# Cross attention's keys and queries as 512-wide paired products, their halves added by VectorE

## The reference, cut to what matters

```python
def cross_attention(h, mem_n, wq, wk, wv, wo):
    b, s, _ = h.shape          # 1, 256, 1024
    m = mem_n.shape[1]         # 256
    q = (h @ wq).reshape(b, s, XATTN_HEADS, XATTN_DIM)      # 4 heads of 256
    k = (mem_n @ wk).reshape(b, m, XATTN_HEADS, XATTN_DIM)
    v = (mem_n @ wv).reshape(b, m, XATTN_HEADS, XATTN_DIM)
    sc = jnp.einsum('bshd,bmhd->bhsm', q, k).astype(jnp.float32) * (XATTN_DIM ** -0.5)
    p = jax.nn.softmax(sc, axis=-1).astype(v.dtype)
    o = jnp.einsum('bhsm,bmhd->bshd', p, v).reshape(b, s, XATTN_HEADS * XATTN_DIM)
    return o @ wo
```

## Time and profile before

| what | value |
|---|---|
| time, median of 3 runs (lowest, highest) | 2178.57 us (2178.45, 2178.62) |
| the profiled execution's own time | 2178.50 us |
| its span in the trace | 2176.6 us |
| TensorE busy | 2161.1 us, 99% of the span |
| VectorE, ScalarE busy | 1475.3 us (68%), 1116.0 us (51%) |
| keys to values, layer by layer | 1339.5 to 1421 us, and 1883.2 to 1965 us |

### The profile page before, as it was taken

The page is one execution under the profiler, slowest core; times in us unless marked ns, Lnnn a source line. Parts: engine busy times, 40 slices in busy tenths (PEclk is TensorE's granted clock), DMA queues, the critical chain, the costliest instruction groups (busy, mean ns, idle before and its releaser), DMA issues.

```text
span 2176.6 us, 31492 instructions
## 1 busy us (share of the span) xinstructions
PE 2161.1 (99%) x13360; PEld 1869.0 (86%) x13360; DVE 1475.3 (68%) x1624; ACT 1116.0 (51%) x1395; POOL 44.7 (2%) x46
## 2 busy tenths in 40 slices
PE   8999999999999999999999999999999999999998
PEld 7998888888999888888898888988889888898887
DVE  6778677655777868666678777456657877745654
ACT  5555565454564565545466535444446653544442
POOL 0000000000000000000000100000000010000000
PEclk9999999999999999999999999999999999999999
DMA  8555564655664456556564445456556444445652
GB/s 277 169 166 169 173 232 155 212 193 172 199 181 158 156 205 211 174 190 207 164 205 128 146 150 161 154 165 195 193 167 208 130 144 152 160 153 167 193 192 77
DMA packets 248754, 380.80 MB, mean 175 GB/s; under 512 B 22495, under 2 KB 158693, under 8 KB 248614
## 3 DMA queue, kind: packets, MB, share of 16 engines
q1 hardware_dynamic: 248614, 378.78, 54.0%
HBM read 372.26 MB, written 1.05 MB: 172 GB/s over the span
## 4 chain that ended last, share of the span: by engine, by line
PE 97%; DVE 1%; issue 1%; ACT 0%; DMA 0%; POOL 0%; DVEq 0%; SPq 0%; POOLq 0%; ACTq 0%
PE ps L652 9%; PE ps L2531 8%; PE ps L790 8%; PE ps L3101 8%; PE ps L2435 7%; PE ps L662 6%; PE ps L2482 5%; PE ps L1122 5%; PE ps L2456 5%; PE ps L2589 4%; PE ps L1025 4%; PE ps L664 3%; PE ps L2458 2%; PE ps L756 2%; PE ps L1043 2%; PE ps L692 2%
## 5 line engine op out<-in xcount | busy, mean ns | idle before, releaser
L3462 DVE TENSOR_TENSOR b_wlo<-b_ring,b_whi 128x2048 fp32r<-128x2048 f32 (+2 forms) x168 | 379.4, 2262 | 107.9 <-ACT b_whi L3126 107.1
L1419 DVE TENSOR_TENSOR a_wlo<-a_ring,a_whi 128x2048 fp32r<-128x2048 f32 (+1 forms) x173 | 392.6, 2273 | 73.8 <-ACT a_whi L1148 73.4
L3126 ACT CAST b_whi<-b_ring 128x2048 fp32r<-128x2048 f32 (+2 forms) x168 | 318.1, 1893 | 202.3 <-PE ps L3101 76.0
L1148 ACT CAST a_whi<-a_ring 128x2048 fp32r<-128x2048 f32 (+1 forms) x173 | 328.7, 1901 | 150.7 <-PE ps L1025 45.2
L652 PE MATMUL ps<-a_nsp,a_whi 128*128 128x256 f32 x1120 | 202.4, 283 | 0.0
L652 PEld LDWEIGHTS ps<-a_nsp,a_whi 128*128 128x128 f32 x1120 | 174.5, 192 | 0.1
L2531 PE MATMUL ps<-b_whi,b_nsp 128*128 128x512 f32 x512 | 170.9, 400 | 0.0
L790 PE MATMUL ps<-a_whi,a_nsp 128*128 128x512 f32 x512 | 162.2, 392 | 0.0
L652 PE MATMUL ps<-a_nsp,a_wlo 128*128 128x256 f32 x560 | 160.2, 286 | 0.0
L662 PE MATMUL ps<-a_nsp,a_whi 128*128 128x512 f32 x576 | 144.5, 393 | 0.0
L662 PEld LDWEIGHTS ps<-a_nsp,a_whi 128*128 128x128 f32 x576 | 103.7, 189 | 18.6
(11 more groups left out here) (609 smaller groups left out, 4437.9 us busy)
## 6 DMA issues: line engine op xcount, KB each, us to landing
a_ring<-in_w_in SPq DMA_DIRECT2D x49, 1024.0 KB, 5.5
b_ring<-in_w_in SPq DMA_DIRECT2D x46, 1024.0 KB, 5.2
a_ring<-in_w_ffn_in SPq DMA_DIRECT2D x44, 1024.0 KB, 5.1
a_ring<-in_w_gate SPq DMA_DIRECT2D x32, 1024.0 KB, 5.4
b_ring<-in_w_up SPq DMA_DIRECT2D x32, 1024.0 KB, 5.7
b_ring<-in_w_down SPq DMA_DIRECT2D x32, 1024.0 KB, 4.9
a_ring<-in_w_ffn_out SPq DMA_DIRECT2D x22, 1024.0 KB, 4.9
a_ring<-in_w_branch SPq DMA_DIRECT2D x16, 1024.0 KB, 5.1
```

Source lines behind the costliest of these rows:

```text
L1148: nc.scalar.copy(high(l, h), raw(l, h)).then_inc(hi_ok, 1)
L1419: nc.vector.tensor_tensor(low(l, h), raw(l, h), high(l, h).bitcast(F32), ALU.subtract).then_inc(lo_ok, 1)
L3126: nc.scalar.copy(high(l, h), raw(l, h)).then_inc(hi_ok, 1)
L3462: nc.vector.tensor_tensor(low(l, h), raw(l, h), high(l, h).bitcast(F32), ALU.subtract).then_inc(lo_ok, 1)
```

## The change

Keys and queries (8 parts in each of the two layers) are made by `apart_block` in place of `feature_block`. For this the memory's low and high halves lie side by side in one tile, `memsp`, as `nsp` has it for x. A part now takes two banks, `PAIR_BANK`: keys 6+7, 4+5, 6+7, 4+5, queries 2+3, 0+1, 2+3, 0+1. ScalarE copies the first halves of both banks as it copied the whole bank before, with the same number of elements, and raises `pair_half`. VectorE adds the second halves with a new instruction, `add_half(j)` (j = 0 to 3 for the keys, 4 to 7 for the queries), and raises `pair_sum`; TensorE's waits, of the scores and of the products that fill a bank again, are now for `pair_sum`. `add_half(0)` stands on VectorE behind `lo(39)`, and `add_half(i - 37)` behind `lo(i + 2)` in the turns 38 to 44.

```diff
-    memhi, memlo = (at(n, [P, KD, SEQ], F32R, offset=base + i) for n, i in (("memhi", 8192), ("memlo", 16384)))
+    memsp = at("memsp", [P, KD, 2 * SEQ], F32R, offset=base + 8192)
+    memlo, memhi = memsp[:, :, 0:SEQ], memsp[:, :, SEQ:2 * SEQ]
...
-    wk_ps, wk_free, qv_ps, qv_free = sem("wk_ps"), sem("wk_free"), sem("qv_ps"), sem("qv_free")
+    wk_ps, pair_sum, qv_ps, qv_free = sem("wk_ps"), sem("wk_free"), sem("qv_ps"), sem("qv_free")
+    pair_half = spe
...
+    PAIR_BANK = (6, 4, 6, 4, 2, 0, 2, 0)
...
         def cross_qk(h):
-            pe.wait_ge(qv_free, h + 1)
-            pe.wait_ge(wk_free, 4)
+            pe.wait_ge(pair_sum, 4 + h + 1)
...
             h = H_WK + i
             pe.wait_ge(lo_ok, h + 1)
-            pe.wait_ge(*((nlo_ok, 8) if i < 2 else (wk_free, i - 1)))
+            pe.wait_ge(*((nlo_ok, 8) if i < 2 else (pair_sum, i - 1)))
             for m in range(2):
-                mm = feature_block(ps[:, 6 + i % 2, m * SEQ:(m + 1) * SEQ], h, m * P, memhi, memlo)
+                mm = apart_block(PAIR_BANK[i] + m, h, m * P, memsp)
...
             h = H_WQ + i
             pe.wait_ge(lo_ok, h + 1)
             if i == 2 or i == 3:
-                pe.wait_ge(qv_free, i - 1)
-            if i == 6:
-                pe.wait_ge(qv_free, 4)
+                pe.wait_ge(pair_sum, 4 + i - 1)
+            if i == 4 or i == 6:
+                pe.wait_ge(pair_sum, 7 + i // 6)
             for m in range(2):
                 if m == 1:
                     cross_mid(h)
                 if i < 4:
-                    mm = feature_block(ps[:, i % 2, m * SEQ:(m + 1) * SEQ], h, m * P, nhi, nlo)
+                    mm = apart_block(PAIR_BANK[4 + i] + m, h, m * P)
                     continue
...
         def wk_out(i):
             act.wait_ge(wk_ps, i + 1)
-            A.copy(xk[:, 2 * i:2 * i + 2, :], ps[:, 6 + i % 2, :].rearrange("p (a b) -> p a b", a=2)
-                   ).then_inc(wk_free, 1)
+            A.copy(xk[:, 2 * i:2 * i + 2, :], ps[:, PAIR_BANK[i]:PAIR_BANK[i] + 2, 0:SEQ]).then_inc(pair_half, 1)
...
+        def add_half(j):
+            out = (xk, xq)[j // 4][:, 2 * (j % 4):2 * (j % 4) + 2, :]
+            dve.wait_ge(pair_half, 2 + j + 1)
+            V.scalar_tensor_tensor(out, ps[:, PAIR_BANK[j]:PAIR_BANK[j] + 2, SEQ:2 * SEQ], (1.0, 256 ** -0.5)[j // 4],
+                                   out, ALU.mult, ALU.add).then_inc(pair_sum, 1)
...
         lo(H_WK + 3)
+        add_half(0)
         for i in range(H_WK + 2, H_UP):
             if i == H_WK + 2:
                 turned(2, 0, QX, nhi, nlo)
             if 42 <= i < 46:
                 cross_norm(i - 42)
             lo(i + 2)
+            if i <= H_WK + 8:
+                add_half(i - 1 - H_WK)
```

More of the change, by code:

```diff
@@ L160 @@
     "wk_ps": 4, "qv_ps": 10, "xs_ps": 4, "up_ps": 16, "dn_used": 15, "hi_ok": 84, "in_ms": 4, "nhi_ok": 24,
-    "ssq_ok": 8, "cq_out": 2, "free_a": 26, "ct_ok": 1, "spe": 2, "mq_ok": 1, "silu_ok": 3, "l2_sq": 1,
+    "ssq_ok": 8, "cq_out": 2, "free_a": 26, "ct_ok": 1, "spe": 10, "mq_ok": 1, "silu_ok": 3, "l2_sq": 1,
     "l2_rt": 1, "le_ok": 4, "ex_ok": 6, "pt_a": 1, "sil_ok": 2, "yh_ok": 4, "eg_ok": 1, "dec_ok": 1, "sig_ok": 2,
-    "x0_ok": 6, "yy_ok": 6, "ms_ok": 6, "mh_ok": 4, "wk_free": 4, "qv_free": 8, "yt_out": 4, "isc_ok": 4,
+    "x0_ok": 6, "yy_ok": 6, "ms_ok": 6, "mh_ok": 4, "wk_free": 8, "qv_free": 4, "yt_out": 4, "isc_ok": 4,
     "up_free": 16, "hh_ok": 16, "par_ok": 1, "lo_ok": 84, "xn_ok": 12, "nlo_ok": 16, "pad_ok": 2, "msq_ok": 4,
@@ L2450, in token_block, with apart_block @@
             return mm
-        def apart_block(bank_, h, c):
+        def apart_block(bank_, h, c, pair=nsp):
             hi, lo = both(h)
             for k in range(KD):
-                T.matmul(ps[:, bank_, :], hi[:, k, c:c + P], nsp[:, k, :], start=k == 0, stop=False)
+                T.matmul(ps[:, bank_, :], hi[:, k, c:c + P], pair[:, k, :], start=k == 0, stop=False)
             for k in range(KD):
-                mm = T.matmul(ps[:, bank_, 0:SEQ], lo[:, k, c:c + P], nhi[:, k, :], start=False, stop=k == KD - 1)
+                mm = T.matmul(ps[:, bank_, 0:SEQ], lo[:, k, c:c + P], pair[:, k, SEQ:2 * SEQ], start=False,
+                              stop=k == KD - 1)
             return mm
@@ L2953, in cross_pv @@
             pe.wait_ge(xpt_ok, h + 1)
-            pe.wait_ge(qv_free, 6 + h // 2 * 2)
+            pe.wait_ge(qv_free, 2 + h // 2 * 2)
             for b in range(2):
@@ L3039, in tensor @@
             if i == 0:
-                pe.wait_ge(qv_free, 8)
+                pe.wait_ge(qv_free, 4)
             residual_rows(H_WO + i, i, 1)
@@ L3265, in qv_out @@
                 act.wait_ge(qv_ps, i + 1)
-                A.activation(xq[:, 2 * i:2 * i + 2, :], ps[:, i % 2, :].rearrange("p (a b) -> p a b", a=2), ACT.Copy,
-                             scale=256 ** -0.5).then_inc(qv_free, 1)
+                A.activation(xq[:, 2 * i:2 * i + 2, :], ps[:, PAIR_BANK[4 + i]:PAIR_BANK[4 + i] + 2, 0:SEQ], ACT.Copy,
+                             scale=256 ** -0.5).then_inc(pair_half, 1)
             elif i % 2:
```

## The result

The changed kernel takes 2219.8 us (median of 4 runs, 2218.7 to 2221.2) where the kernel before takes 2178.6: a ratio of 1.0189, 95% interval 1.0177 to 1.0201. It is slower by 41 us. The profiled execution took 2218.7 us against 2178.5, so 40.2 us have to be found in the trace. The forecast was 2215.4.

The account below looks back on a forecast made before the run. TensorE was taken as the bound. To 2178.5 us, 29.4 were added for waits less matmul savings (2207.9), then 7.5 for three clock falls: 2215.4 us, range 2206.0 to 2221.0.

Parts of the forecast that it names:

- Bound: Whole kernel: TensorE, busy 99% of the span, bounds it; each microsecond of matmul removed is gained, each waited is lost.
- Matmuls, 2.6 us: Key and query blocks of the cross attention: 2.80 us in place of 2.88, saving 2.6 us in both layers.
- VectorE's and ScalarE's time at nothing: ScalarE's copies unchanged, VectorE's additions 5.5 us a layer: both cost nothing by themselves; only the additions' place in order costs.
- K3's wait, 1.0 us: TensorE, before key product K3, stands still 1.0 us a layer for K1's sum behind part 40's low half.
- The scores' waits, 5.9, 4.5 and 4.6 us: TensorE, before scores of heads 1, 2, 3, waits that long in each layer for the sums of Q1, Q2, Q3.
- The sum without the clock, 2207.9: Whole kernel: 2178.5 us plus 29.4 for both layers' waits less matmul savings, before any clock fall.
- The clock: TensorE after long pauses: falls to half rate, 2.5 us each; three falls counted, 7.5 us.
- I count one of them: Of the four 4.5 us pauses, one brings a clock fall; with both 5.9 us pauses, three falls.
- (B): Rival: TensorE's clock holds or falls once at most; 2207.9, up to 2210.4 us; chance 0.30.
- (C): Rival: not slower, VectorE's sums are ready in time; 2175.9 us; chance 0.03.
- (D): Rival: products not made as the diff says, or 512-wide two-bank blocks slower, say 0.2 us each; 2221.8 us; chance 0.04.

Follow-up runs that it names:

- The filled pauses: Changed kernel plus useless 512-column matmuls ahead of the waits for the scores of heads 1, 2 and 3 (22, 16, 16): 2208.33 us.
- the first experiment: Changed kernel with the sums of K1 to K3 and Q0 to Q3 moved on VectorE ahead of norm and low half: 2175.72 us, ratio 0.9987.

## Why the prediction was right, point by point

- **Bound.** Right: TensorE was the bound, and the pauses and the savings came through nearly in full. The pauses, from start to start, are 2 x (1.0 + 5.9 + 4.5 + 4.5) = 31.8 us; less 2.8 for the matmuls and with 10.4 for the falls that is 39.4 of the 40.2 us.
- **Matmuls, 2.6 us.** Right: 2.79 us a block, and 2.8 us in all in the kernel with the sums first.
- **VectorE's and ScalarE's time at nothing.** Right: twice the work at the sums changed nothing. The sum takes 0.687 us, the row of the up projection said 0.692.
- **K3's wait, 1.0 us.** Right: 0.85 us shown in the trace, 1.0 from start to start.
- **The scores' waits, 5.9, 4.5 and 4.6 us.** Right: from start to start 5.9, 4.5 and 4.5. The round read off the rows of the kernel before (8.7 and 7.35 us) held to within 0.1, since its links were there already and had only to be put in a row. One of its parts was tested by itself: with the low half taken away each pause shrank by 2.2.
- **The sum without the clock, 2207.9.** The filled pauses measured it: 2208.3.
- **The clock.** The mechanism was right, its two numbers were not. The step that failed is the count of falls, "I count one of them": three were taken and there were six, each followed by scores of 3.2 to 3.8 us. It was set by a single row, the 4.7 us at the program's start, as if that were a limit; the runs show falls from 2.14 us on. The price of one was mis-sized the other way, 2.5 us against (2218.7 - 2208.3) / 6 = 1.73 on average. The single falls cost 1.6 to 2.2 us, by the time between two scores with and without filled pauses. The stretch at the start that I took has 5.5 us of slow work; behind the six pauses the clock was back after 3.1 to 4.5 us of work. That the start is the same effect isn't shown either, as the granted clock reads full there. Six falls cost 10.4 us where I had 3 x 2.5 = 7.5, and the forecast came out 3.3 us low in the profiled execution, 4.4 in the median. That it lies this near is in part luck: the two errors offset each other, and six falls at my own price would have been 2222.9, above the range. The second layer's fall is in the slice at 1946 and not around 1929 as written, for I had not added there what the first layer loses.
- **The rivals.** The clock that holds (B) is refuted by the clock's row, and by the filled pauses, which are that case made real. That the sums are in time (C) is what the first experiment brought about; it gave 2175.7 for the 2175.9 written there. A costlier paired form (D) is refuted by the 2.79 us.

## What to carry to other kernels

When an engine's result gets a second stage on another engine, read what stands ahead of that stage in the second engine's order and what each of these instructions waits for; here a 0.69 us sum stood behind a chain that began only with the next product's end, and moving it was worth 44 us. Put the instruction that releases the bound engine ahead of those that nobody waits for yet, even if they are older. A pause of a TensorE that is otherwise never idle can cost more than its length: here the six in the changed kernel cost 1.7 us each on top, on average.

## What the runs showed of the hardware

From the one profiled execution of each kernel, the pauses for a sum in the changed kernel, in the one with the queries' sums first, the one with them behind the norm and the two with filled pauses, and the speed of what followed:

| pause as shown, us | cases | with a fall to 1.2 GHz in it or right behind it |
|---|---|---|
| 0.69 to 0.85 | 16 | 0 |
| 1.65 | 2 | 0 |
| 2.14 to 2.18 | 4 | 1 |
| 2.50 | 2 | 1 |
| 3.48 to 3.56 | 4 | 4 |
| 4.34 to 5.76 | 6 | 6 |

The clock can also fall when the work has begun again. In the changed kernel, before the scores of head 2 (idle until 1400.06, busy from there):

```profile
1399.00:1400.00 1.00, 0.00 (x0) 1.00 0.00 0
1400.00:1401.00 1.00, 0.94 (x4) 0.85 0.00 0
1401.00:1403.00 2.00, 2.00 (x6) 0.50 0.00 0
```

All of this pause of 4.34 us passed at 2.4 GHz; the fall to 1.2 GHz came with the first matmuls behind it. So a clock that is still full at a pause's end did not mean full speed behind it here. Why one pause of 2.14 us brought a fall and another, at the same place of the other layer, did not, the runs leave open.

The Trainium skill, page "TensorE: Matmul & The Clock Gate", section "Part 1: The HAM clock gate", says that idleness sends the array to half rate and that the phase of its observation is not bound to the program. The traces agree on the first: none of the ten pauses of 3.48 us or more was spared. That equal pauses of 2.14 us ended differently fits the second, but no run here shows the phase. The page was the better guide to the count than the one row that I used.
